# Conv, silu and q/k norms of the gated-delta pairs, made ahead in small turns beside other pairs

## What is computed

```
full = concat([conv_buf, qkv]);  conv = full[:, 0:T]*conv_w[0]
for j in 1..3: conv = conv + full[:, j:j+T]*conv_w[j]
q, k, v = split(silu(conv), 3)
q = l2norm(heads(q)) * HEAD_DIM**-0.5;  k = l2norm(heads(k))
beta = sigmoid(b_logit);  g = -exp(a_log)*softplus(a_logit + dt_bias)
o, S = gdn_chunked(q, k, v, g, beta, S0)      # chunked triangular solve and recurrence
```

## Time and profile before

| | us |
|---|---|
| median of 3 runs | 2929.69 (2923.2 to 2931.07) |
| the profiled execution, its own time | 2920.97 |
| its span | 2918.8 |
| TensorE busy | 2690.9 (92%) |
| VectorE busy | 1668.0 (57%) |
| ScalarE busy | 947.2 (32%) |
| mean granted TensorE clock | 0.929 |

### The profile page before, as it was taken

One profiled execution on the slowest core, in us unless ns is written; L12 is line 12 of the kernel. 1 busy time (PEld: TensorE's weight loads), 2 busy tenths in 40 slices (PEclk: granted clock), 3 DMA queues, 4 the chain that ended last, 5 costly groups with the idle time before them and its releaser, 6 DMA issues.

```text
span 2918.8 us, 59294 instructions
## 1 busy us (share of the span) xinstructions
PE 2690.9 (92%) x23238; PEld 2517.7 (86%) x23238; DVE 1668.0 (57%) x2503; ACT 947.2 (32%) x1694; POOL 161.0 (6%) x168
## 2 busy tenths in 40 slices
PE   8999999978897989999999999999787888999996
PEld 8999998866665889999999999988666667999996
DVE  5666337654646466663366653566455655666534
ACT  4333224332222243332233332333222223333323
POOL 1030110000000010001100001100000001000011
PEclk9999999977877999999999999999786789999998
DMA  4853334200000322222222233431000021222321
GB/s 109 107 88 87 88 93 130 65 24 6 9 9 4 103 68 86 86 86 85 79 83 86 86 88 88 124 102 49 14 2 9 9 70 54 80 86 86 88 89 56
DMA packets 380501, 201.67 MB, mean 69 GB/s; under 512 B 41461, under 2 KB 376821, under 8 KB 379528
## 3 DMA queue, kind: packets, MB, share of 16 engines
q1 hardware_dynamic: 377928, 197.46, 23.5%
q0 software_dynamic: 2400, 1.82, 1.9%
HBM read 188.07 MB, written 13.34 MB: 69 GB/s over the span
## 4 chain that ended last, share of the span: by engine, by line
PE 78%; DVE 10%; issue 5%; ACT 5%; DMA 1%; SPq 1%; DVEq 0%; POOLq 0%; ACTq 0%; POOL 0%
PE ps L682 53%; PE ps L737 23%; DVE ar L1925 3%; ACT ar L1420 2%; DVE ar L1919 2%; DVE wl L1803 1%; ACT wh L1351 1%; SPq L529 1%; PE ps L1011 1%; DMA raws<-in_ffn_w_in 0%; DVE x L1919 0%; DVE xl L1910 0%; DVE ar L1955 0%; DVE ar L1922 0%; DMA raws<-in_w_in 0%
## 5 line engine op out<-in xcount | busy, mean ns | idle before, releaser
L1803 DVE TENSOR_TENSOR wl<-raws,wh 128x1024 fp32r<-128x1024 f32 x336 | 411.2, 1225 | 672.9 <-ACT wh L1351 668.5
L682 PE MATMUL ps<-xh,wh 128*128 128x272 f32 x2880 | 604.9, 292 | 18.0 <-DVE wl L1803 15.5
L682 PE MATMUL ps<-xh,wl 128*128 128x272 f32 x2880 | 600.0, 290 | 0.0
L682 PE MATMUL ps<-xl,wh 128*128 128x272 f32 x2880 | 598.7, 289 | 0.0
L737 PE MATMUL ps<-ar 64*64 64x64 f32 (+13 forms) x5408 | 478.3, 276 | 130.5 <-ACT ar L1420 38.9
L737 PEld LDWEIGHTS ps<-ar 64*64 64x64 f32 (+6 forms) x5408 | 358.2, 163 | 226.0 <-issue 62.9
L1351 ACT ACTIVATE wh<-raws 128x1024 fp32r<-128x1024 f32 x336 | 354.8, 1057 | 418.4 <-PE ps L682 377.2
L682 PEld LDWEIGHTS ps<-xh,wh 128*128 128x128 f32 x2880 | 457.7, 190 | 21.8 <-DVE wl L1803 18.2
L682 PEld LDWEIGHTS ps<-xl,wh 128*128 128x128 f32 x2880 | 458.1, 190 | 0.0
L682 PEld LDWEIGHTS ps<-xh,wl 128*128 128x128 f32 x2880 | 457.6, 190 | 0.0
L682 PE MATMUL ps<-hh,wh 128*128 128x272 f32 x1408 | 292.2, 289 | 0.0
(11 more groups left out here) (190 smaller groups left out, 2721.1 us busy)
## 6 DMA issues: line engine op xcount, KB each, us to landing
raws<-in_ffn_w_in SPq DMA_DIRECT2D x176, 512.0 KB, 3.7
raws<-in_ffn_w_out SPq DMA_DIRECT2D x64, 512.0 KB, 4.0
raws<-in_w_in SPq DMA_DIRECT2D x42, 512.0 KB, 3.6
raws<-in_ffn_w_out SPq DMA_DIRECT2D x32, 384.0 KB, 3.4
raws<-in_w_out SPq DMA_DIRECT2D x16, 448.0 KB, 4.1
x_kept<-x SPq DMA_DIRECT2D x2, 2176.0 KB, 10.1
x<-x_kept SPq DMA_DIRECT2D x2, 2176.0 KB, 8.0
ar<-in_consts SPq DMA_DIRECT2D x2, 1337.5 KB, 6.7
```

Source lines behind the costliest of these rows:

```text
L682: ins = pe.matmul(ps[:, bank + h, 0:n1 - h * NH], w[u % 2][:, k, :], a[:, k0 + k, h * NH:n1], start=(first and k == 0 and n == 0), stop=(l ...
L1803: dve.tensor_tensor(wl[u % 2][:, :, :], raw[u % 2][:, :, :], wh[u % 2][:, :, :].bitcast(F32), ALU.subtract).then_inc(sem("wl_done"), 1)
```

## The change

Conv, silu and squares of pair 2 are made in 16 turns in the first period, those of pair 3 in 16 turns in the second (convolve, on VectorE, ScalarE and TensorE). Their results W lie in unused chunks of xh and xl (chunks 1 and 6 for pair 2; 6 and 7 for pair 3; tanh results in chunk 0 and in V_CH of proj), and the norm sums and roots in dead chunks of proj (sq, y). The turns of VectorE are 4 taps for each of q, k, v, then 3 silu products and an empty turn. ScalarE has a tanh in its turns 5, 9 and 13 and the two Squares in turn 15. The norm sums of pair 2 stand on TensorE in the first step of prepare(1) and its roots on ScalarE in the gates' first step, the Newton steps on VectorE after prepare(1)'s prep. For pair 3 the sums and the roots stand at the head of prepare(2), the Newton steps after its masks. prepare_gdn shrinks to 26 and 25 steps: beta_b moves ahead of ge's products, the large dif behind the small one and behind the read of beta (kk_read), and the minima and masks behind prep. alternate() takes any number of generators, each with a fraction at which it begins.

```diff
-PREPARE_STEPS = (27, 27 + GATE_STEPS, 30, 30)
+PREPARE_STEPS = (27, 27 + GATE_STEPS, 26, 25)
+CONV_STEPS = 16
...
+    order = sorted((begin + (1 - begin) * (k + 1) / n, t) for t, (_, n, begin) in enumerate(turns) for k in range(n))
...
+    alternate((samples_attend(), SAMPLE_STEPS, 0), (prepare(0), PREPARE_STEPS[0], 0), (convolve(pairs[2]), CONV_STEPS, 1 / SAMPLE_STEPS))
+    alternate((prepare(1), PREPARE_STEPS[1], 0), (finish(0), FINISH_STEPS, 0), (convolve(pairs[3]), CONV_STEPS, 0))
+    for q in (1, 2):
+        alternate((prepare(q + 1), PREPARE_STEPS[q + 1], 0), (finish(q), FINISH_STEPS, 0))
...
 (TensorE)
+                def norm_sums_of(p):
+                    pe.wait_ge(sem("qk_sq"), at(lay, "qk_sq", 2 * (p.c + 1)))
...
+                    for k in range(2):
+                        mm(ps[:, 1 + k, :], cst("blk"), p.sq[:, k, 0:SEQ])
+                    for k in range(2):
+                        ins = mm(ps[:, 3, k * NSAMP:(k + 1) * NSAMP], cst("blk"), p.sq[:, k, SEQ:NT])
...
                         ins.then_inc(*tick("gates_t"))
+                        norm_sums_of(pairs[2])
                         for _ in range(GATE_STEPS - 1):
                             yield
                         pe.wait_ge(sem("gate_in"), at(lay, "gate_in", 2))
+                        pe.wait_ge(sem("qk_out"), at(lay, "qk_out", 1))
...
                     banks_free(q)
+                    if q == 2:
+                        norm_sums_of(pairs[3])
+                        yield
+                        pe.wait_ge(sem("qk_out"), at(lay, "qk_out", 2))
+                    pe.wait_ge(sem("beta"), at(lay, "beta", 1))
+                    for h in range(2):
+                        ins = mm(ps[:, 2 + h, 0:NH], cst("sel", 8)[:, c * P:(c + 1) * P], proj[0:8, BA_CH, h * NH:(h + 1) * NH])
+                    ins.then_inc(*tick("beta_b"))
...
 (ScalarE)
                     go(proj[0:8, BA_CH, :], proj[0:8, BA_CH, :], ACT.Tanh, scale=0.5).then_inc(*tick("gate_e"))
+                    norm_roots(pairs[2])
...
+                def norm_roots(p):
+                    act.wait_ge(sem("qk_sum"), at(lay, "qk_sum", p.c + 1))
...
+                    go(p.sq[:, :, 0:SEQ], ps[:, 1:3, :])
+                    go(p.sq[:, :, SEQ:NT], sums)
+                    go(p.y[:, :, SEQ:NT], sums, ACT.Ln, bias=eps_l2).then_inc(*tick("a_ln"))
+                    go(p.y[:, :, 0:SEQ], ps[:, 1:3, :], ACT.Ln, bias=eps_l2).then_inc(*tick("qk_out"))
...
+                    go(p.y, p.y, ACT.Exp, scale=-0.5).then_inc(*tick("rs_exp"))
...
 (VectorE)
+                def convolve(p):
...
+                    for j in range(3):
+                        for k in range(4):
+                            if k:
+                                dve.wait_ge(sem("conv"), last(lay, "conv"))
+                            tap(p, k, j)
+                            yield
+                    dve.wait_ge(sem("conv"), last(lay, "conv"))
+                    for j in range(3):
+                        conv_silu(p, j)
+                        yield
+                    yield
...
+                    if q == 1:
+                        newton(pairs[2].y, pairs[2].sq, L2_EPS, pairs[2].sq, "rs_exp", "d_seq", 2)
```

More of the change, by code:

```diff
@@ L188, in run, with alternate, head_pairs @@
         pass
[L191 to L204, removed]
+def alternate(*turns):
+    order = sorted((begin + (1 - begin) * (k + 1) / n, t) for t, (_, n, begin) in enumerate(turns) for k in range(n))
+    for _, t in order:
+        next(turns[t][0])
+    assert all(next(steps, None) is None for steps, _, _ in turns)
+def head_pairs(prepare, finish, samples_attend, convolve, mix, pairs):
+    alternate((samples_attend(), SAMPLE_STEPS, 0), (prepare(0), PREPARE_STEPS[0], 0), (convolve(pairs[2]), CONV_STEPS, 1 / SAMPLE_STEPS))
+    alternate((prepare(1), PREPARE_STEPS[1], 0), (finish(0), FINISH_STEPS, 0), (convolve(pairs[3]), CONV_STEPS, 0))
+    for q in (1, 2):
+        alternate((prepare(q + 1), PREPARE_STEPS[q + 1], 0), (finish(q), FINISH_STEPS, 0))
+    alternate((mix(), MIX_STEPS, 0), (finish(3), FINISH_STEPS, 0))
 ORDER = tuple(range(SCH, SCH + 6)) + tuple(range(0, SCH)) + tuple(range(GCH, PC))
@@ L982, in prepare_gdn @@
                     yield
+                    pe.wait_ge(sem("kk_read"), at(lay, "kk_read", q + 1))
+                    for i in range(TILES):
+                        for hp in range(2):
+                            g = ge[:, i, hp * HD:hp * HD + 1].broadcast_to([P, P])
+                            dst = ps[:, 2 + i // 2, (i % 2 * 2 + hp) * P:(i % 2 * 2 + hp + 1) * P]
+                            mm(dst, g, cst("gd")[:, 0:P], stop=False)
+                            ins = mm(dst, cst("neg_incl"), g, start=False)
+                    ins.then_inc(*tick("dif"))
                     yield
@@ L1274, in mix @@
                     yield
-                head_pairs(prepare, finish, samples_attend, mix)
+                head_pairs(prepare, finish, samples_attend, convolve, mix, pairs)
                 pe.wait_ge(sem("head_l"), at(lay, "head_l", 4))
@@ L2205, in prepare_gdn @@
                     dve.sem_inc(*tick("ge"))
-                    dve.wait_ge(sem("xe"), at(lay, "xe", 1))
-                    for k in range(3):
-                        tap(k)
-                        dve.wait_ge(sem("d_seq"), last(lay, "d_seq"))
+                    stt(U[:, K_, :], p.W[1], 0.5, p.y[:, 1, :], ALU.mult, ALU.mult).then_inc(*tick("d_seq"))
+                    dve.wait_ge(sem("beta_b"), at(lay, "beta_b", c + 1))
+                    stt(halves(U[:, BV, :]), halves(p.W[2]), 0.5, bank2(2), ALU.mult, ALU.mult).then_inc(*tick("d_seq"))
```

180 lines of the change are left out of this document (90 added, 90 removed).

## The result

| | before | after |
|---|---|---|
| median, us (6 runs of each, in turns) | 2926.02 (2922.31 to 2931.07) | 2949.71 (2941.34 to 2960.78) |
| the profiled execution, its own time | 2920.97 | 2953.97 |

The changed kernel is slower: ratio 1.008, 95% interval 1.0057 to 1.0103. I had forecast 2916.7, and the range ended at 2942. The medians are 23.7 us apart.

A forecast was written before the change was run, and what follows sets the result against it. VectorE and ScalarE were taken to bound the heads of periods 2 and 3, TensorE waiting. Per layer +3 + 4 + 9.5 - 7 - 16 = -6.5 us, two layers -13: median 2916.7 us, range 2895 to 2942.

The forecast's parts named there:

- Heads of periods 2 and 3: Start of periods 2 and 3: first transpose about 28 and 15 us after the start, instead of 36 and 34.
- two owed finish steps: At the grams: finish steps still left over, some 1.1 and 2 us in period 3, 3 to 6 us in period 2.
- the terms -7 and -16: Net change a layer from earlier grams: period 2 -7 us (ends -4, -10), period 3 -16 us (ends -14, -18).
- case C: Periods 2 and 3: shorter waiting stretch lets TensorE stay at full clock; -11.5 us a layer, 2906.7; chance 0.2.
- half clock throughout: Periods 2 and 3: the poor ends, with TensorE never at full clock, -4 and -14 us a layer.
- Case D: Head stage: finish steps once hidden by convolution become the wait; +2.5 us a layer or less, 2930 to 2935; chance 0.2.
- Period 0: the turns: 12 taps and 3 silu products added in period 0, mostly in VectorE's waits: +3 us a layer, ends +1 and +6.
- Period 1, the turns: Pair 3's turns and pair 2's Newton steps added in period 1: +4 us a layer, ends +2 and +8.
- Period 1, ScalarE's block: Pair 2's norm roots ahead of the gates' Exp in period 1 delay VectorE's gates: +9.5 us a layer, ends +7, +11.
- Period 4: The period after period 3: no term in the sum, forecast change 0.
- Case B: Inverses of periods 0 and 1: turns break TensorE-VectorE exchange, TensorE at half clock; +6.7 us a layer, 2943.1; chance 0.15.
- signs that I had named for being wrong: Period 1 growing under 8, periods 2 and 3 together shrinking over 30, inverse levels of 0/1 growing over 1 us.

## Why the prediction was wrong

**Heads of periods 2 and 3: right.** First transposes 16.6 and 23.0 us behind the start of the period; I had said 15 and 28. The masks of pair 3's grams start 15.9 us earlier (24.4 us behind the period's start against 40.3), those of pair 2 14.1 us (31.5 against 45.6), where I had 7 to 13.

**The rest of periods 2 and 3: the step that failed.** I ended the sum at the grams, and took what lies behind them as it was, apart from two owed finish steps. The rest of period 3 went from 37.9 to 52.0 us: idle plus full is 37.9 in both, lost 0.0 and 14.1. All of it is the clock. The rest of period 2 went from 52.4 to 64.2: idle -1.1, full +3.5 (the owed steps, of which I had 3 to 6 us), lost +9.4. In period 2 the half clock was moved rather than added: its head lost 10.5 us less than before (4.5 against 15.0), and the rest took nearly as much. So the terms -7 and -16 became -2.4 and -1.7. That case C or half clock throughout might come, I had written, but priced both within the head alone: +3 and +2 us for half clock. The granted clock of the rest stood in the trace of before, at 1.00, and was an asset to be costed like the cover of a hidden step.

**Case D was right that the gain is eaten,** but not by its mechanism, and its 2930 to 2935 was short. Its +20.5 for periods 0 and 1 was near (+19.7 in layer 0); its -18 for periods 2 and 3 was not (-4.1 and -6.9). The waits behind the grams of period 3 are hardly longer (idle 6.3 and 6.6 us), and the same order of steps gives period 3 76.4 us in one kernel and 68.9 in another.

**Case C was wrong in its direction.** A shorter stretch of waits did not keep the clock up: TensorE is at 0.50 from 923.5 to 941.5 though busy for 16.07 of 18 us. The Trainium skill (TensorE: Matmul & The Clock Gate, The HAM clock gate) says "the default state is throttled, and activity releases the throttle"; this trace does not bear that out for these products, busy yet at 0.50, and in the prediction I let it speak for C. That is with busy time taken as activity; what the chip itself counts, no run here shows.

**Period 0: the turns cost +3, measured -0.6** (73.1 against 73.7 us; 73.1 with the turns alone). The wrong step was to charge each turn its length less 0.4 us; the exchange between TensorE and VectorE in pair 0's inverse had room for all of them.

**Period 1, the turns: +4, measured +10.4 and +11.5.** The turns' own length hardly counts (idle +1.7, full -1.2, together less than my 4); the clock was left out (lost +10.0). Dealt out early they cost 3.7 and 5.4.

**Period 1, ScalarE's block: +9.5, measured +9.3 at the place** (707.10 against 697.79; I had 707.3), and 6.1 of these come back when it is moved behind the gates. The mechanism and its length at the place were right. That the whole came near is in part luck: the norm alone costs 11.2 us in layer 0, but as idle +4.3 and full +1.7, so a third of my 9.5 was covered after all, and 5.3 of lost clock, which I did not have, filled it up again (+4.5, +2.1 and +3.6 in layer 1).

**Period 4** I had at nothing; it is +3.6 and +3.3, of which lost is 4.0 (5.9 against 1.9).

In one line for layer 0, periods 1 to 4: idle plus full -8.0 against my -9.5, lost +28.0 against my 0. The first pair agrees mostly because two misses cancel: period 1 came 4.9 us below my term and period 2 5.8 above it.

**Case B** asked for +1 us in each inverse level by broken exchange. What came is of its kind (TensorE at half clock), but it struck in periods 1, 3 and 4 and left period 0 untouched. The level that I had read as half clock ran at 0.62 (680.25 to 685.03), so the 4.78 us were no pure case of it. None of the signs that I had named for being wrong caught the failure: period 1 grew by more than 8 us, and periods 2 and 3 shrank by far less than 30.

What stays open: why the clock comes back after a few us in one kernel and after 20 in the next, and whether the 5 to 14 us of clock that the rest of period 3 loses in every version of the change could be had back. The rows show when it was granted and what TensorE did before; no run here isolates what makes the difference, and period 1 of one and the same kernel differs by up to 4.3 us between the layers (97.3 and 101.6).

## What to carry to other kernels

Split each stretch into TensorE's idle time, its work at full clock and what half clock adds; cost an edit in all three, and ask of the stretch behind it, if it runs at 1.00 now, what would take that away. Put preparatory work behind, not ahead of, the short operation that another engine waits for. A wait that can't be removed may be worth filling with throwaway products (here they gave back the stretch right behind the wait, not the one after it), but only while it is a wait: the same 16 fillers cost 7.12 us in line once it was gone.

## What the runs showed of the hardware

- TensorE stayed at 0.50 through 18 us of which it was busy 16.07 (923.5 to 941.5 of the changed kernel), while in the kernel before it held 1.00 through 30 us with busy shares between 5.13 and 6.00 of each 6.
- Adding work made the changed kernel faster: with 44 filler products a layer its median is 18.3 us lower, and with eight alone a period of 76.4 us became one of 68.1. Two edits that add no work brought the same period to 68.9.
- The scatter between executions of one kernel goes with the clock: of 23 of the kernel before, the shortest (span 2914.4 us) was granted 0.931, the longest (2939.0) 0.921.
- Edits that each helped alone did not add: the early turns were worth -6.7 us without the norm in the period and +3.2 with it.
- On ScalarE each table load took 1.28 us and the activation behind it began 0.01 to 0.02 us later (701.77 + 1.28, then 703.07). Between the Ln and the Exp behind it stood a load (703.07 to 705.75). So the drain that the prediction names beside the load does not show; the changed kernel has two more loads in period 1 and two fewer in period 3, as forecast.
